# The cumulated decay of the SSD chunks: stored once per sequence and read back by broadcast, in place of matmuls

## The chip, the core and the metric

One NeuronCore of a Trainium2 chip runs the kernel. It has a matrix engine (TensorE, PE in the profile), a vector engine (VectorE, DVE), a scalar engine (ScalarE, ACT), GpSimd (POOL) and SyncE (SP), which here only issues transfers. Each engine runs its own list of instructions in order and waits on semaphores. SBUF is the on-chip memory of 128 partitions, PSUM holds 8 banks for the results of matmuls, and DRAM tensors lie outside. The metric is the time of one execution in microseconds of device time, less is better.

## The reference, cut to what matters

The model is one layer of an encoder on two sequences of 512 tokens: a mixing part (SSD heads, neighbourhood attention, pooling), cross attention and a mixture of experts. The change touches the SSD only, a scan over 4 chunks of 128 tokens per sequence, in both directions. For one direction:

```python
la = (dt * a).reshape(b, nc, L, G, R)
cs = jnp.cumsum(la, axis=2)
seg = cs[:, :, :, None] - cs[:, :, None, :]
decay = jnp.exp(jnp.where(tri[None, None, :, :, None, None], seg, -jnp.inf))
cb = jnp.einsum('bclgn,bcsgn->bclsg', cc, bc)
y_diag = jnp.einsum('bclsg,bclsgr,bcsgrp->bclgrp', cb, decay, xdt)
```

For every chunk, direction (2) and head (8), `decay` is a 128 by 128 matrix: the exponential of the cumulated sum at token l minus that at token s. The partitions of a tile hold s. So every partition needs the whole row of `cs` over l, for each head.

## The kernel before, in words

The program is one list of steps, `TL`, built by `timeline()`. Each engine walks the same list in the same order and issues its own part of each step, so an engine's order of work is fixed by the list. A step is a tuple: its kind, the sequence `s` and the chunk or tile.

The steps around the change:
- `dtv`, `dt`: from the projected time steps come `dts` and `la`, then by matmuls the cumulated sums `cs` (tokens on partitions) and totals `tot`. `la` is kept as two parts, `laH` and `laL`, whose sum it is.
- `sback`: the backward states, one step per chunk from the last one down.
- `sdec`: the decay matrices of one chunk. PE first makes the product of `bT` and `cT` (L1039). Then come 32 matmuls (L1047): with `laH` or `laL` of one head, repeated over 128 columns, as the stationary operand and a triangle of ones as the moving one, they leave the cumulated row of this head in every partition of a bank. 8 heads, 2 directions, 2 parts. DVE takes the smaller of that and its own partition's `cs` (L1899), writes `dec`, ACT applies `Exp` (L1530), DVE multiplies by the product `cbm` (L1907).
- `sy`: the output of the chunk. PE multiplies `dec` with `xdt` (L1077) into a bank; DVE adds the parts into `y1` (L1839 to L1875); ACT squares, POOL makes the reciprocal root (`yms`, `yrs`), DVE scales (L1879).
- `sout`: PE transposes, DVE scales into `y1` (L1914), POOL stores it to `mix_scratch`. The next chunk's L1839 waits for that store to land.

The chunks of the first sequence are interleaved with the projections `qk` of the second one, those of the second with the memory projections `mk`, `mv` and the output projection. Such a projection (GEMM in this text) is 24 matmuls of 512 columns on PE (L909 to L911); its `hn1` step is followed by a square on ACT, a sum on DVE (`hss`, L1730), a root on POOL (`hrs`) and a scaling on DVE (L1740). Weights come through `raw`: ACT rounds them into `Wh`, DVE makes the rest `Wl` (L1705).

Banks are given out in turn: each use takes the next of the 8, and PE waits until the use 8 before it is released. A `sdec` step has 6 uses, 4 of them for L1047.

POOL issues its DMAs on its own queue in the order of its steps: in `sdec` it multiplies `xs` with `dts` (`xdt`, L2343), loads the gate `zg` and makes `xw` (L740). The gate was stored in the `z` steps.

Of the kernel before, what the change touches and what calls it, by code (L numbers as in the profile page):

```python
# [23 lines left out]
P = 128  # L24
# [154 lines left out]
def bank_uses(step):  # L179
# [14 lines left out]
    if kind == "sdec":  # L194
        return 6
# [96 lines left out]
def encoder_layer(nc, dram, out):  # L292
# [3 lines left out]
    with ctx:  # L296
# [13 lines left out]
        mix_dram = nc.dram_tensor("mix_scratch", (NT, P, KT, P), F32).ap()  # L310
        z_dram = nc.dram_tensor("gate_scratch", (NT, P, D_INNER), F32).ap()
# [154 lines left out]
        stk.close()  # L466
        oneh_p = nc.alloc_sbuf_tensor_at("oneh_p", [P, 2 * NT, P], BF16, offset=at["raw0"])
# [77 lines left out]
        x_st = [sem(f"x_st{i}") for i in range(NT)]  # L545
# [76 lines left out]
        z_st = [sem(f"z_st{i}") for i in range(NT)]  # L622
# [14 lines left out]
        t_done = sem("t_done")  # L637
        y_done = sem("y_done")
# [267 lines left out]
        def _(pe):  # L906
# [39 lines left out]
            for step in TL:  # L946
# [67 lines left out]
                elif kind == "dt":  # L1014
# [17 lines left out]
                elif kind == "sdec":  # L1032
# [8 lines left out]
                    for dr in range(2):  # L1041
                        for hh in range(2):
                            b = take(pe, step, 2 + 2 * dr + hh)
                            for h in range(4):
                                e = dr * 8 + hh * 4 + h
                                for j, a in enumerate((laH, laL)):
                                    last = pe.matmul(b[:, h * P:(h + 1) * P], a[:, c, e:e + 1].to_broadcast([P, P]),  # L1047
                                                     tri_r[:, dr, :], start=j == 0, stop=j == 1)
                            last.then_inc(is_full(step, 2 + 2 * dr + hh), 1)
                elif kind == "sy":  # L1050
# [23 lines left out]
                    for h in range(SSD_H):  # L1074
                        hc = slice(h * SSD_P, (h + 1) * SSD_P)
                        for dr in range(2):
                            last = pe.matmul(b[:, hc], dec[:, dr, h, :], xdt[:, dr, hc], start=dr == 0, stop=dr == 1)  # L1077
# [251 lines left out]
        def _(act):  # L1329
# [34 lines left out]
            def stored(i):  # L1364

                for j in range(i, i + 4):
                    act.wait_ge(x_st[j], 16)
# [10 lines left out]
            for step in TL:  # L1378
# [19 lines left out]
                elif kind == "norm":  # L1398
# [18 lines left out]
                    if st == "ffn":  # L1417
                        act.dma_start(px_dram[i * P:(i + 1) * P, :], x_sb[:, i, :]).then_inc(x_st[i], 16)
# [105 lines left out]
                elif kind == "sdec":  # L1524
                    s, c = step[1], step[2]
                    for dr in range(2):
                        for hh in range(2):
                            wait_released(act, step, 2 + 2 * dr + hh)
                            for h in range(4 * hh, 4 * hh + 4):
                                last = act.activation(dec[:, dr, h, :], dec[:, dr, h, :], ACT.Exp,  # L1530
                                                      bias=ncs[:, dr, c, h:h + 1])
# [108 lines left out]
        def _(dve):  # L1640
# [49 lines left out]
            for step in TL:  # L1690
# [96 lines left out]
                elif kind == "z":  # L1787
                    k = nth(*step)
                    dve.wait_ge(zt_done, k + 1)
                    if k:  # L1790
                        dve.wait_ge(z_st[k - 1], 16)
# [21 lines left out]
                elif kind == "dt":  # L1813
                    k = nth(*step)
# [66 lines left out]
                elif kind == "sdec":  # L1881
# [10 lines left out]
                    if k:  # L1892
                        wait_full(dve, ("sy",) + chunks[k - 1], 0)
                    for dr in range(2):
                        for g in range(SSD_G):

                            j = 2 + 2 * dr + g
                            wait_full(dve, step, j)
                            tt(dec[:, dr, 4 * g:4 * g + 4, :], pb(step, j)[:, :].rearrange("p (h l) -> p h l", h=4),  # L1899
                               per_head(cs[:, dr, c, 4 * g:4 * g + 4], P), ALU.min).then_inc(is_free(step, j), 1)  # L1900
                    for g in range(SSD_G):
                        wait_released(dve, step, g)
                    for dr in range(2):
                        for g in range(SSD_G):
                            dve.wait_ge(e_done, 4 * k + 2 * dr + g + 1)
                            d = dec[:, dr, 4 * g:4 * g + 4, :]
# [315 lines left out]
        def _(pool):  # L2222
# [18 lines left out]

            pool.memset(neghalf[:, :], -0.5)
# [266 lines left out]
```

## Time and profile before

| what | us |
|---|---|
| median of 3 runs | 1236.51 (1230.76 to 1240.05) |
| the profiled execution, its own time | 1230.7 |
| its span | 1228.7 |
| PE busy | 1038.7 (85% of the span), 5029 instructions recorded |
| PE, loading of weights | 819.1 (67%) |
| DVE busy | 782.6 (64%) |
| ACT busy | 468.8 (38%) |
| POOL busy | 298.6 (24%) |

A busy share says how long an engine had something in work, not whether anybody waited for it. The profile also gives PE's granted clock (1.00 is 2.4 GHz, 0.50 is 1.2 GHz; mean 0.926 here), the share of the DMA engines, and for each instruction the idle time before it with what ended that time. "<-issue" means that nothing in the profile was waited for.

### The profile page before, as it was taken

The page shows a single profiled execution, that of the slowest core. Times are in us where ns is not written, and L with a number is a line of the kernel's source. Part 1 is how long each engine was busy: PE and PEld are TensorE (multiplying, and loading weights), DVE is VectorE, ACT ScalarE, POOL GpSimd, SP SyncE. Part 2 cuts the span into 40 slices and gives each one's busy share as a digit, 9 for nine tenths or more (in the row PEclk, how much of TensorE's full clock was granted, in tenths as well). Part 3 has the DMA queues.
Part 4 walks back from the last instruction along what each step waited for, and adds up shares of the span by engine and source line. Part 5 has one row for each costly group of instructions (what it writes and reads, how often), then busy time and mean ns, then how long its engine had stood idle before and what let it go on. Part 6 is the DMA issues. An engine that isn't in the chain of part 4 may idle for free.

```text
span 1228.7 us, 13980 instructions
## 1 busy us (share of the span) xinstructions
PE 1038.7 (85%) x5029; PEld 819.1 (67%) x5029; DVE 782.6 (64%) x1251; ACT 468.8 (38%) x849; POOL 298.6 (24%) x346
## 2 busy tenths in 40 slices
PE   1878978989797898999996999974999988898884
PEld 1746766867576677788875777764777666676662
DVE  4435766787566666774245466655898777877781
ACT  4222335233223523331113333323565655565560
POOL 1203402331340232110011111112244333232322
PEclk9988988879898896988988999976999999999998
DMA  5122223022122322433131001463699999899973
GB/s 190 37 70 84 77 96 122 18 70 78 60 78 86 117 73 86 146 103 129 60 91 35 35 35 52 163 282 125 224 367 367 362 354 355 348 360 361 347 281 102
DMA packets 65124, 197.40 MB, mean 161 GB/s; under 512 B 16608, under 2 KB 23168, under 8 KB 52640
## 3 DMA queue, kind: packets, MB, share of 16 engines
q1 hardware_dynamic: 43520, 151.14, 34.0%
q0 software_dynamic: 18688, 39.52, 9.0%
q10 hardware_dynamic: 2848, 5.84, 1.3%
q8 instruction: 41, 0.67, 0.2%
q14 instruction: 27, 0.22, 0.1%
HBM read 190.16 MB, written 37.75 MB: 185 GB/s over the span
## 4 chain that ended last, share of the span: by engine, by line
PE 44%; DVE 18%; issue 13%; DMA 11%; ACT 8%; POOL 6%; ACTq 1%; SPq 0%; DVEq 0%; POOLq 0%
DMA edr<-w_e_down 9%; PE bank L909 8%; PE bank L910 8%; PE bank L911 8%; DVE egl L1687 3%; PE gu_ps L909 2%; PE gu_ps L911 2%; PE gu_ps L910 2%; PE bank L959 2%; PE y_ps L1272 2%; DVE x_sb L1780 1%; DVE xn L1714 1%; DVE Wl L1705 1%; PE bank L1163 1%; ACT ghi L1362 1%
## 5 line engine op out<-in xcount | busy, mean ns | idle before, releaser
L909 PE MATMUL bank<-Wh,hTh 128*128 128x512 f32 x384 | 162.8, 424 | 4.6 <-issue 4.6
L910 PE MATMUL bank<-Wl,hTh 128*128 128x512 f32 x384 | 157.4, 410 | 0.0
L911 PE MATMUL bank<-Wh,hTl 128*128 128x512 f32 x384 | 156.7, 408 | 0.0
L1687 DVE TENSOR_TENSOR egl<-egr,ghi 128x2048 fp32r<-128x2048 f32 x64 | 144.1, 2291 | 14.9 <-ACT ghi L1362 14.9
L1362 ACT ACTIVATE ghi<-egr 128x2048 fp32r<-128x2048 f32 x64 | 119.6, 1931 | 0.0
L909 PE MATMUL gu_ps<-ghi,xgH 128*128 128x512 f32 x256 | 103.5, 404 | 1.4 <-DVE xgL L2054 1.4
L1705 DVE TENSOR_TENSOR Wl<-raw,Wh 128x1024 fp32r<-128x1024 f32 (+1 forms) x64 | 77.4, 1217 | 38.6 <-ACT Wh L1362 38.4
L911 PE MATMUL gu_ps<-ghi,xgL 128*128 128x512 f32 x256 | 100.7, 394 | 0.0
L910 PE MATMUL gu_ps<-egl,xgH 128*128 128x512 f32 x256 | 100.2, 392 | 0.0
L909 PEld LDWEIGHTS bank<-Wh,hTh 128*128 128x128 f32 x384 | 78.1, 203 | 22.6 <-issue 6.6
L911 PEld LDWEIGHTS bank<-Wh,hTl 128*128 128x128 f32 x384 | 76.9, 200 | 17.5
L910 PEld LDWEIGHTS bank<-Wl,hTh 128*128 128x128 f32 x384 | 77.4, 202 | 15.9
L1362 ACT ACTIVATE dhi<-edr 128x1024 fp32r<-128x1024 f32 x32 | 33.9, 1060 | 134.2 <-DMA edr<-w_e_down 118.0
L909 PE MATMUL bank<-hTh,Wh 128*128 128x512 f32 (+1 forms) x176 | 74.9, 425 | 9.2 <-issue 8.3
L1362 ACT ACTIVATE Wh<-raw 128x1024 fp32r<-128x1024 f32 (+1 forms) x64 | 63.1, 999 | 30.5 <-PE bank L911 19.6
L959 PE MATMUL bank<-ident,xn 128*128 128x128 f32 x160 | 29.5, 345 | 53.2 <-DVE xn L1714 53.2
L911 PE MATMUL bank<-hTh,Wl 128*128 128x512 f32 (+1 forms) x176 | 72.7, 413 | 0.0
L910 PE MATMUL bank<-hTl,Wh 128*128 128x512 f32 (+1 forms) x176 | 72.6, 413 | 0.0
L2059 DVE TENSOR_TENSOR edl<-edr,dhi 128x1024 fp32r<-128x1024 f32 x32 | 39.1, 1223 | 48.4 <-ACT dhi L1362 48.3
L2371 POOL DMA_INDIRECT pg<-partial_rows,idh x32 | 51.7, 1616 | 64.6 <-DMA partial_rows<-pg,idh 61.9
L2376 POOL DMA_INDIRECT partial_rows<-pg,idh x28 | 33.1, 1182 | 141.3 <-DVE pg L2079 141.3
L1272 PE MATMUL y_ps<-edr,hbF 128*128 128x512 f32 x128 | 65.3, 591 | 0.0
(309 smaller groups left out, 2190.6 us busy)
## 6 DMA issues: line engine op xcount, KB each, us to landing
egr<-w_e_gate SPq DMA_DIRECT2D x32, 1024.0 KB, 17.7
egr<-w_e_up SPq DMA_DIRECT2D x32, 1024.0 KB, 21.0
edr<-w_e_down SPq DMA_DIRECT2D x32, 1024.0 KB, 14.3
raw<-w_in SPq DMA_DIRECT2D x72, 256.0 KB, 3.0
raw<-w_xkv SPq DMA_DIRECT2D x16, 256.0 KB, 3.1
raw<-w_out SPq DMA_DIRECT2D x16, 256.0 KB, 3.2
raw<-mix_scratch SPq DMA_DIRECT2D x16, 256.0 KB, 3.4
partial_rows<-x_sb ACTq DMA_DIRECT2D x8, 512.0 KB, 2.7
```

The costliest lines, as they stand in the source:

```text
L909: pe.matmul(dst, ah, bh, start=first, stop=False)
L910: pe.matmul(dst, ah, bl, start=False, stop=False)
L911: return pe.matmul(dst, al, bh, start=False, stop=last)
L959: last = pe.transpose(b[:, j * P:(j + 1) * P], NORMED[st][0][:, f * P:(f + 1) * P], ident[:, :])
L1163: last = pe.matmul(b[:, j * 256:(j + 1) * 256], xqT[:, h, :], xkT[:, h, s * N_MEM:(s + 1) * N_MEM], start=True, stop=True)
L1272: last = pe.matmul(y_ps[:, c], hbF[:, :], edr[n % 3][:, 1, c], start=False, stop=True)
L1362: return act.activation(dst, src, ACT.Copy, **kw)
L1687: tt(egl[n % 4][:, a, :, :], egr[n % 4][:, a, :, :], ghi[n % 2][:, a, :, :].bitcast(F32), ALU.subtract)\
L1705: tt(lo, src, h, ALU.subtract).then_inc(w_low, 1)
L2059: tt(edl[n % 3][:, 0, :], edr[n % 3][:, 0, :], dhi[n % 2][:, 0, :].bitcast(F32), ALU.subtract)\
L2371: return pool.indirect_dma_start(out=to, out_offset=None, in_=table, in_offset=bass.IndirectOffsetOnAxis(ap=idx, axis=0), bounds_check=bou ...
L2376: return pool.indirect_dma_start(out=table, out_offset=bass.IndirectOffsetOnAxis(ap=idx, axis=0), in_=frm, in_offset=None, bounds_check=bo ...
```

## The change

The cumulated sums are produced a second time, now with heads on partitions, and travel through DRAM.
- `dt`: four more matmuls (128 columns each) leave the cumulated rows of all 4 chunks, 8 heads and one direction in 64 partitions. DVE copies them to `y1`, POOL stores them to `decay_scratch` (64 KB).
- `sdec`: the 32 matmuls and their 4 banks are gone. One DMA from POOL per chunk (`load_decay`) reads the chunk's 16 rows of 128 numbers and writes them to all 128 partitions of a tile, 8 KB a partition, 1 MB in all. Two tiles `decays` alternate; the second lies over `prob`, which the neighbourhood attention uses at other times. DVE's `min` now works in place on that tile.
- POOL issues the loads of chunks 0 and 1 in the step `sback` of chunk 1, the loads of chunks 2 and 3 in `sdec` of chunks 1 and 2, ahead of `xdt`.
- Semaphores of the stores of `z` and of the rows for the experts are shared by two tiles each, so that there are enough of them.

```diff
@@ bank_uses
     if kind == "sdec":
-        return 6
+        return 2
@@ encoder_layer
+        cs_dram = nc.dram_tensor("decay_scratch", (SEQS, 2, TPS * 2 * SSD_H, P), F32).ap()
+        decays = [dec, nc.alloc_sbuf_tensor_at("dec1", [P, 2, SSD_H, P], F32, offset=at["prob"])]
@@ PE, dt
+                    for dr in range(2):
+                        for j, a in enumerate((laH, laL)):
+                            last = pe.matmul(b[0:64, 128 + dr * P:256 + dr * P], a[:, :, :].rearrange("p c h -> p (c h)"),
+                                             tri_r[:, dr, :], start=j == 0, stop=j == 1)
                     last.then_inc(is_full(step), 1)
@@ PE, sdec
-                    for dr in range(2):
-                        for hh in range(2):
-                            b = take(pe, step, 2 + 2 * dr + hh)
-                            for h in range(4):
-                                e = dr * 8 + hh * 4 + h
-                                for j, a in enumerate((laH, laL)):
-                                    last = pe.matmul(b[:, h * P:(h + 1) * P], a[:, c, e:e + 1].to_broadcast([P, P]),
-                                                     tri_r[:, dr, :], start=j == 0, stop=j == 1)
-                            last.then_inc(is_full(step, 2 + 2 * dr + hh), 1)
@@ DVE, dt
+                    if s:
+                        dve.wait_ge(ssd_st[s - 1], 16 * TPS)
+                    dve.tensor_copy(y1[0:64, 0:2 * P], b[0:64, P:3 * P]).then_inc(cst_done, 1)
@@ DVE, sdec
-                    if k:
-                        wait_full(dve, ("sy",) + chunks[k - 1], 0)
+                    dve.wait_ge(dec_ld[c % 2], 16 * (k // 2 + 1))
                     for dr in range(2):
                         for g in range(SSD_G):
-
-                            j = 2 + 2 * dr + g
-                            wait_full(dve, step, j)
-                            tt(dec[:, dr, 4 * g:4 * g + 4, :], pb(step, j)[:, :].rearrange("p (h l) -> p h l", h=4),
-                               per_head(cs[:, dr, c, 4 * g:4 * g + 4], P), ALU.min).then_inc(is_free(step, j), 1)
+                            d = decays[c % 2][:, dr, 4 * g:4 * g + 4, :]
+                            tt(d, d, per_head(cs[:, dr, c, 4 * g:4 * g + 4], P), ALU.min).then_inc(min_done, 1)
@@ POOL
+            def load_decay(s, c):
+
+                rows_of = bass.AP(cs_dram.tensor, (P * s + 2 * SSD_H * c) * P, [[0, P], [(64 + SSD_H) * P, 2], [1, SSD_H * P]])
+                pool.dma_start(decays[c % 2][:, :, :, :].rearrange("p d h l -> p d (h l)"), rows_of)\
+                    .then_inc(dec_ld[c % 2], 16)
@@ POOL, steps
+                elif kind == "dt":
+                    pool.wait_ge(cst_done, step[1] + 1)
+                    pool.dma_start(cs_dram[step[1]].rearrange("d r l -> r d l"),
+                                   y1[0:64, 0:2 * P].rearrange("p (d l) -> p d l", d=2)).then_inc(cs_st, 16)
...
-                elif kind == "sback" and step[2] > 1:
-                    decayed(pool, step[1], 1, step[2] - 1, per_head, heads)
+                elif kind == "sback":
+                    s, c = step[1], step[2]
+                    if c > 1:
+                        decayed(pool, s, 1, c - 1, per_head, heads)
+                    else:
+                        if s:
+                            wait_full(pool, ("sy", s - 1, TPS - 1), 0)
+                        pool.wait_ge(cs_st, 16 * (s + 1))
+                        load_decay(s, 0)
+                        wait_full(pool, ("nav", s, 3))
+                        load_decay(s, 1)
...
+                    if 0 < c < TPS - 1:
+                        load_decay(s, c + 1)
```

What stands on POOL before chunk 0 of the first sequence: the load of `gain`, the root `hrs` of the projection norm, then the step's own work. Before:

```order
L2261 DMA gain<-norm_mem 128x1024
L2233 TENSOR_SCALAR hms<-hss 128x8
L2234 TENSOR_TENSOR hrs<-hms,neghalf 128x8
L2343 TENSOR_TENSOR xdt<-x_sb,dts 128x512 x2
L2346 DMA x_sb<-gate_scratch 128x512
L740 TENSOR_TENSOR xw<-x_sb,wst 128x512
```

And now, in the numbering of the changed kernel (`dec_49` is the second tile):

```order
L2269 DMA gain<-norm_mem 128x1024
L2235 TENSOR_SCALAR hms<-hss 128x8
L2236 TENSOR_TENSOR hrs<-hms,neghalf 128x8
L2247 DMA dec<-decay_scratch 128x2x1024
L2247 DMA dec_49<-decay_scratch 128x2x1024
L2366 TENSOR_TENSOR xdt<-x_sb,dts 128x512 x2
L2369 DMA x_sb<-gate_scratch 128x512
L746 TENSOR_TENSOR xw<-x_sb,wst 128x512
```

The two loads stand behind `hrs` and ahead of `xdt`. The second place on POOL is chunk 2 of the first sequence, behind the root `yrs` of chunk 1. Before:

```order
L2233 TENSOR_SCALAR yms<-yss 128x2
L2234 TENSOR_TENSOR yrs<-yms,neghalf 128x2
L2343 TENSOR_TENSOR xdt<-x_sb,dts 128x512 x2
L2346 DMA x_sb<-gate_scratch 128x512
L740 TENSOR_TENSOR xw<-x_sb,wst 128x512
```

Now:

```order
L2235 TENSOR_SCALAR yms<-yss 128x2
L2236 TENSOR_TENSOR yrs<-yms,neghalf 128x2
L2247 DMA dec_49<-decay_scratch 128x2x1024
L2366 TENSOR_TENSOR xdt<-x_sb,dts 128x512 x2
L2369 DMA x_sb<-gate_scratch 128x512
L746 TENSOR_TENSOR xw<-x_sb,wst 128x512
```

The load of chunk 3 came in between `yrs` and `xdt`. The third place is PE at chunk 1 of the second sequence. Now the product of `bT` and `cT`, the transposes of chunk 0's output and the next GEMM follow each other:

```order
L977 MATMUL bank<-ident,qn 128x128 x8
L1049 MATMUL bank<-x_sb 128x128 x2
L1084 MATMUL bank<-ident,y 128x128 x4
L915 MATMUL bank<-Wh,hTh 128x512
L916 MATMUL bank<-Wl,hTh 128x512
```

Before, the 32 matmuls of L1047 stood between the second and the third of these rows, ending so:

```order
L1047 MATMUL bank<-tri_r,laH 128x128
L1047 MATMUL bank<-tri_r,laL 128x128
L1083 MATMUL bank<-ident,y 128x128 x4
L909 MATMUL bank<-Wh,hTh 128x512
L910 MATMUL bank<-Wl,hTh 128x512
```

The GEMM moved up by these 32 instructions.

## Rows read from the trace of the kernel before

**Rows 1.** Two stretches: us, busy us (instructions) of PE, PEld, DVE, ACT, POOL; clock; DMA
```profile
205.00:320.00 115.00, 101.33 (x556) 80.47 (x557) 83.46 (x177) 34.63 (x100) 32.23 (x41) 0.88 0.22 65
420.00:560.00 140.00, 129.05 (x653) 106.55 (x652) 97.82 (x166) 46.00 (x111) 30.71 (x40) 0.88 0.31 102
```

**Rows 2.** What is recorded on line 1047, and who waited for it (us, times)
```profile
L1047 PE MATMUL bank<-tri_r,laH x128: 272/274/476, 214.7 to 544.3; 128*128 128x128 f32 x128
...
  DVE dec L1899: 2.8, 3
```

**Rows 3.** PE in order of time, first chunk: start, us, instruction, idle before
```profile
214.69 0.33 PE L1047 MATMUL bank<-tri_r,laH 128*128 128x128 f32 x1
...
218.21 0.27 PE L1047 MATMUL bank<-tri_r,laL 128*128 128x128 f32 x1
...
227.81 4.91 PE L1077 MATMUL bank<-xdt,dec 128*128 128x64 f32 x32 [1.24 <-DVE dec L1907]
```

**Rows 4.** DVE in order of time, first sequence
```profile
221.52 2.48 DVE L1899 TENSOR_TENSOR dec<-bank,cs 128x512 f32<-128x512 f32 x4
...
227.06 0.69 DVE L1907 TENSOR_TENSOR dec<-dec,cbm 128x512 f32<-128x512 f32 x1 [0.47 <-ACT dec L1530]
...
240.61 0.61 DVE L1879 TENSOR_SCALAR y<-y,yrs 128x256 f32<-128x256 f32 x2 [2.04 <-POOL yrs L2234]
241.14 0.68 DVE L1730 TENSOR_REDUCE hss<-sqb 128x8 f32<-128x512 f32 x1
...
246.13 2.47 DVE L1899 TENSOR_TENSOR dec<-bank,cs 128x512 f32<-128x512 f32 x4
...
266.50 2.17 DVE L1879 TENSOR_SCALAR y<-y,yrs 128x256 f32<-128x256 f32 x2 [2.04 <-POOL yrs L2234]
```

**Rows 5.** POOL in order of time, first sequence
```profile
215.26 1.67 POOL L2234 TENSOR_TENSOR hrs<-hms,neghalf 128x8 f32<-128x8 f32 x1
...
246.91 1.06 POOL L740 TENSOR_TENSOR xw<-x_sb,wst 128x512 f32<-128x512 f32 x1
...
266.44 2.08 POOL L2343 TENSOR_TENSOR xdt<-x_sb,dts 128x512 f32<-128x512 f32 x2
```

**Rows 6.** DMA issues from 205 to 222 us: count, KB each, median us to landing
```profile
gain<-norm_mem POOLq DMA_DIRECT2D x1, 512.0 KB, 5.2
...
x_sb<-gate_scratch POOLq DMA_DIRECT2D x1, 256.0 KB, 3.1
```

**Rows 7.** Tile egr: all 64 loads of 1 MB, issue to landing
```profile
DMA to landing us min/median/max: 4.8/18.2/24.3
```

**Rows 8.** PE in order of time, second sequence
```profile
482.21 0.78 PE L909 MATMUL bank<-Wh,hTh 128*128 128x512 f32 x1
...
522.57 6.01 PE L1077 MATMUL bank<-xdt,dec 128*128 128x64 f32 x32 [3.36 <-DVE dec L1907]
...
552.52 5.32 PE L1077 MATMUL bank<-xdt,dec 128*128 128x64 f32 x32 [1.26 <-DVE dec L1907]
```

**Rows 9.** DVE in order of time, second sequence
```profile
450.49 2.48 DVE L1899 TENSOR_TENSOR dec<-bank,cs 128x512 f32<-128x512 f32 x4
...
481.72 0.69 DVE L1899 TENSOR_TENSOR dec<-bank,cs 128x512 f32<-128x512 f32 x1 [1.02 <-PE bank L1047]
...
491.41 1.23 DVE L1705 TENSOR_TENSOR Wl<-raw,Wh 128x1024 fp32r<-128x1024 f32 x1 [5.55 <-ACT Wh L1362]
492.55 0.42 DVE L1839 TENSOR_TENSOR y<-bank,ecs 128x256 f32<-128x256 f32 x1
...
565.10 0.69 DVE L1977 TENSOR_TENSOR x_sb<-x_sb,bank 128x512 f32<-128x512 f32 x1 [2.01 <-PE bank L911]
```

**Rows 10.** POOL in order of time, second sequence
```profile
442.40 1.01 POOL L2234 TENSOR_TENSOR hrs<-hms,neghalf 128x4 f32<-128x4 f32 x1
...
486.15 0.59 POOL L2359 DMA_DIRECT2D mix_scratch<-y  x1 [9.14 <-DVE y L1914]
```

**Rows 11.** PE in order of time, after the `dt` step
```profile
194.11 1.97 PE L959 MATMUL bank<-ident,xn 128*128 128x128 f32 x8 [2.42 <-DVE xn L1714]
```

More of the change, by code:

```diff
@@ L544, in encoder_layer @@
         count_done = sem("count_done")
-        x_st = [sem(f"x_st{i}") for i in range(NT)]
+        x_st = [sem(f"x_st{i}") for i in range(TPS)]
         eg_ld = [[sem(f"eg_ld{i}{a}") for a in range(2)] for i in range(4)]
@@ L621, in encoder_layer @@
         zg_done = sem("zg_done")
-        z_st = [sem(f"z_st{i}") for i in range(NT)]
+        z_st = [sem(f"z_st{i}") for i in range(TPS)]
         z_ld = sem("z_ld")
@@ L637, in encoder_layer @@
         t_done = sem("t_done")
+        cst_done = sem("cst_done")
+        cs_st = sem("cs_st")
+        dec_ld = [sem(f"dec_ld{i}") for i in range(2)]
+        min_done = sem("min_done")
         y_done = sem("y_done")
@@ L1076, in _ @@
                         for dr in range(2):
-                            last = pe.matmul(b[:, hc], dec[:, dr, h, :], xdt[:, dr, hc], start=dr == 0, stop=dr == 1)
+                            last = pe.matmul(b[:, hc], decays[c % 2][:, dr, h, :], xdt[:, dr, hc], start=dr == 0, stop=dr == 1)
                     last.then_inc(is_full(step, 0), 1)
@@ L1417, in _ @@
                     if st == "ffn":
-                        act.dma_start(px_dram[i * P:(i + 1) * P, :], x_sb[:, i, :]).then_inc(x_st[i], 16)
+                        if i >= TPS:
+                            act.wait_ge(x_st[i - TPS], 16)
+                        act.dma_start(px_dram[i * P:(i + 1) * P, :], x_sb[:, i, :]).then_inc(x_st[i % TPS], 16)
                 elif kind == "hT" and step[1] == "ffn":
@@ L1527, in _ @@
                         for hh in range(2):
-                            wait_released(act, step, 2 + 2 * dr + hh)
+                            act.wait_ge(min_done, 4 * nth(*step) + 2 * dr + hh + 1)
                             for h in range(4 * hh, 4 * hh + 4):
-                                last = act.activation(dec[:, dr, h, :], dec[:, dr, h, :], ACT.Exp,
-                                                      bias=ncs[:, dr, c, h:h + 1])
+                                d = decays[c % 2][:, dr, h, :]
+                                last = act.activation(d, d, ACT.Exp, bias=ncs[:, dr, c, h:h + 1])
                             last.then_inc(e_done, 1)
@@ L1813, in _ @@
                 elif kind == "dt":
-                    k = nth(*step)
+                    k, s = nth(*step), step[1]
                     wait_full(dve, step)
@@ L2336, in _ @@
                     k = nth(*step)
-                    pool.wait_ge(z_st[k], 16)
-                    pool.wait_ge(z_st[s * TPS + TPS - 1], 16)
+                    pool.wait_ge(z_st[c], 16 * (s + 1))
+                    pool.wait_ge(z_st[TPS - 1], 16 * (s + 1))
                     if k:
@@ L2407, in _ @@
             for i in range(NT):
[L2408 removed]
+                pool.wait_ge(x_st[i % TPS], 16 * (i // TPS + 1))
             gather_rows(2)
```

9 lines of the change are left out of this document (4 added, 5 removed).

## The prediction, made before the changed kernel ran

> **What bounds the kernel now.** I read the busy table of two stretches first: 205 to 320 us, where the first sequence's SSD chunks run, and 420 to 560 us, where the second's do [rows 1]. PE is busy 101.3 of 115.0 and 129.1 of 140.0 us there, DVE 83.5 and 97.8. That looks like PE as the bound, and the change takes PE work away. So the next view asks who waits for that work. Line 1047 holds 256 matmuls (two groups of 128), and in the whole execution DVE waits for them 2.8 us, in three pieces [rows 2]. Then I follow one chunk in order of time. The 32 matmuls of chunk 0 start between 214.69 and 218.21, 0.11 us apart. PE later reaches L1077, sits idle 1.24 us for DVE's L1907, and starts at 227.81, right when DVE's last L1907 ends (227.06 + 0.69) [rows 3, 4]. From 221.52 to 241.14 no idle time of DVE is put down to PE: its gaps are 0.47 us for ACT's exponentials and 2.04 us for ACT's squares and POOL's square root [rows 4]. So in the first sequence each chunk is one long chain DVE, ACT, POOL, DVE, in DVE's fixed order, and PE fills the time beside it. Taking work from PE there buys idle PE.
>
> **What is removed.** At that spacing, 3.52 us for 31 steps, the 256 matmuls take at least 29 us of PE. On the path are only the places where DVE waits. All are in chunk 1 of the second sequence. L1899 waits for line 1047 three times, 2.8 us in all, the last time 1.02 [rows 2, 9]. With these waits gone, L1907 will wait for ACT twice as in chunk 0, 0.47 us each [rows 4], which it doesn't there now: 1.8 us are left. Behind the same matmuls stands the GEMM that starts at 482.21 [rows 8]. It starts about 6 us earlier without them (they run at the low clock there, and DVE's `Wl` becomes its wait), so ACT's `Wh` comes earlier and DVE's wait of 5.55 us before 491.41 closes [rows 9]. What is late next is the store of `y1`: issued at 486.15 [rows 10], now 1.8 earlier, at 484.3; with 3.1 us to landing, as another 256 KB on this queue [rows 6], it lets L1839 start at 487.4, where it starts at 492.55 now [rows 9]. Gain: **5.2 us**.
>
> **What is added, and where it is hidden.** The four extra matmuls and DVE's copy of the cumulated decay in the `dt` step cost nothing. The transpose behind them has 2.42 us idle before it, waiting for `xn` [rows 11], and four matmuls of 128 columns at 0.11 to 0.21 us are under 0.9. If the cover were gone, each of the two steps would cost that. The store of `decay_scratch` has over 10 us until its first reader. `min` reads SBUF in place of PSUM with the same 512 elements a partition: nothing by itself.
>
> **The first load of each sequence.** It stands on POOL behind the square root `hrs` of the projection norm. In the first sequence that ends at 215.26 + 1.67 = 216.93 [rows 5], and DVE wants the tile at 221.52 [rows 4]: 4.6 us. In the second it ends at 443.41 [rows 10] and DVE wants it at 450.49 [rows 9]: 7.1 us. No row shows a broadcast of 1 MB on POOL's queue. The nearest is `gain`, the same 4 KB row to 128 partitions, 512 KB, 5.2 us to landing; a 256 KB load takes 3.1 [rows 6]. Going on at that slope gives 9.4. From below, the fastest 1 MB load, plain and on SP's queue, took 4.8 [rows 7]. I take 7.0, nearer to the broadcast row plus 512 KB at its pace. Then DVE waits **2.4 us** in the first sequence (0.2 to 4.8) and **0** in the second (0 to 2.3). The loads of chunks 1 to 3 are issued some 20 us before use. As a page has it (the Trainium skill, "DMA: Bandwidth & Descriptors", section "Anatomy of one DMA — SWDGE (gpsimd) path"), a transfer costs about 2.0 us plus its bytes at 436 GB/s, 4.4 us for 1 MB as an estimate. By that the first wait would be nil and the sum 2.4 us lower.
>
> **PE's clock.** With more idle time before L1077, PE will run it low. L1077 took 4.91 us after 1.24 us of idling [rows 3], 5.32 after 1.26, but 6.01 after 3.36 [rows 8]. After the change PE idles there for 1.24 us, the 3.5 of the matmuls and the wait for the load, 5 to 7 us. This costs where the path goes on through PE: in chunk 0 the GEMM behind L1077 feeds ACT and then L1730 at 241.14, which follows L1879 (240.61 + 0.61) without a gap [rows 4]; ACT's square before it waited for that GEMM, so I count no slack. I take 6.0: **1.1 us** in the first sequence, 0.9 in the second's chunk 0, and 0.7 in its chunk 3, where L1977 at 565.10 waits for PE [rows 9]. From below 0; from above, 32 steps at half the pace of 0.11 us (7.0) give 2.1, 1.9 and 1.7.
>
> **POOL and DVE beside each other.** A DVE instruction can be held up by POOL: two L1879 take 0.61 us at 240.61, but 2.17 at 266.50, where POOL's `xdt` starts at 266.44 [rows 4, 5]. In chunk 2 the new load's issue (about 0.6 us, as 486.15 shows [rows 10]) stands between `yrs` and `xdt`, so L1879 runs free: 1.6 us back in each sequence. But DVE meets `xdt` and `xw` one instruction later. I take half, **0.8 us gained** each (0 to 1.6). In chunk 1 `xdt` and `xw` move 0.6 us later, onto L1899. Today L1899 takes 2.47 us at 246.13 with `xw` beside it [rows 4, 5], as much as the 2.48 without it at 221.52: by this row the price is nil. But its source was a bank, and L1879's, in SBUF, was held up 1.6. So 0 to 2 us; I take **1.0** in each sequence. The Trainium skill ("SBUF — State Buffer", section "Who interferes with whom") says that a DVE instruction with two SBUF inputs contends with a GpSimd instruction that reads SBUF, and one with at most one does not (outside certain modes). It speaks against this change, since L1899 gets a second SBUF input. By the rule the 1.0 stays, by the row of L1899 alone the sum would be 2.0 lower.
>
> **The sum.** First sequence: 2.4 + 1.1 + 1.0 - 0.8 = +3.7. Second: 0.9 + 1.0 - 5.2 - 0.8 + 0.7 = -3.4. Together +0.3 us: 29 us of PE time or more leave and the span stays. What follows hangs on the chain and moves along. Against the profiled run's own time, 1230.7 us (span 1228.7), this is 1231.0. The median of the runs shown, 1236.5, is 5.8 above that run, so I say 1236.8, about **1237**. All lower ends: first -1.4, second -5.2 - 1.6 = -6.8, so 1228.3. All upper ends: first 4.8 + 2.1 + 2.0 = 8.9; second 2.3 + 1.9 + 2.0 - 5.2 + 1.7 = 2.7, so 1248.1.
>
> **The rivals.**
> - Load in time: the load lands within 4.8 us and the clock costs nothing. For it: SP's fastest 1 MB. Against: the broadcast row with half the bytes took longer. Sum about -8: 1228.
> - PE's time is on the path after all: 29 us come off, 1208. For it: PE is busy for 88 and 92% of the stretches. Against: 2.8 us of waiting in all.
> - Slower, by one mechanism: the broadcast read. All 128 partitions fetch the same 8 KB, and if these reads queue up, the load lands late at both first chunks. Each us beyond 7 costs one in each sequence, so the kernel is 1% slower from 13 us to landing: 1249. For it: no row of this size. Against: `gain`'s 5.2 us.
>
> **How the numbers follow.** The forecast has 0.58, load in time 0.18, PE on the path 0.08, a queueing broadcast 0.16. About 1%, 12.4 us, is what a measurement of this kernel can tell from no change. PE on the path gives faster, with a share of the load in time: 0.11. The slow load passes 1% for most of its chance: 0.14. The rest, 0.75, is within 1%. The runs shown lie between 1230.8 and 1240.1, so a median moves by a few us as well: 1227 to 1249 takes in both sums of ends and leaves out what is beyond 1% on either side.
>
> **What would show it.** In the new profile: L1899 of chunk 0 waits for a DMA, 2 to 3 us in the first sequence and near none in the second; L1077 takes 6 us or more in most chunks; the share of PE falls by over 2 points with the span as it was; the L1879 behind the load of chunk 3 takes 0.6 us; the 5.55 us before L1705 is gone. The prediction is wrong if the stretch from 205 to 320 us gets shorter, if DVE waits for later loads too, or if DVE's time for L1899 grows by more than 1 us a chunk.

## The result and the profile after

The changed kernel takes 1239.8 us (median of 20 runs, 1236.0 to 1246.1), the kernel before, measured beside it, 1233.4 us (20 runs, 1225.6 to 1241.8). The ratio is 1.0054, 95% interval 1.0031 to 1.0076. A second measurement of 12 runs gave 1.0052 (1.0029 to 1.0074). So the change costs about 6 us: half a per cent, less than the 1% below which I counted it as no change, and yet real.

| | before | after |
|---|---|---|
| span of the profiled execution, us | 1228.7 | 1239.3 |
| PE busy, us | 1038.7 | 1018.4 |
| DVE busy, us | 782.6 | 792.5 |
| POOL busy, us | 298.6 | 319.7 |
| mean granted clock | 0.926 | 0.909 |

PE lost 20 us of busy time and the span got longer. The same stretches as in [rows 1], in the kernel after (us, busy us of PE, PEld, DVE, ACT, POOL, clock, DMA share, GB/s):

```profile
205.00:320.00 115.00, 85.11 (x399) 65.02 (x399) 87.49 (x173) 33.64 (x98) 32.82 (x43) 0.79 0.29 95
420.00:560.00 140.00, 114.23 (x526) 91.91 (x527) 101.87 (x173) 48.79 (x118) 35.46 (x47) 0.85 0.40 139
```

PE has 16.2 us less in the first stretch, at a clock of 0.79 in place of 0.88. DVE has 4.0 us more. It has the same arithmetic, but for one small copy per sequence that lies ahead of this stretch, so something holds its instructions up. To find where, I put the two traces side by side by DVE's order and took, for each of its instructions, start after minus start before. That difference is -1.86 us at 204 us (mostly chance: a second trace of the same kernel before stands at -1.99 there), +5.2 at 320, +4.9 at 430 and +4.3 at 600. So 7.1 us are lost in the first sequence's chunks, and 0.7 won in the second's. The steps of the difference stand at few instructions. DVE after, first sequence (start, us, instruction; lines are 2 to 6 higher than before):

```profile
215.73 3.20 DVE L1867 TENSOR_TENSOR S_b<-S_b,edec 64x256 f32<-64x256 f32 x2
...
221.04 2.48 DVE L1902 TENSOR_TENSOR dec<-dec,cs 128x512 f32<-128x512 f32 x4
...
242.58 0.69 DVE L1733 TENSOR_REDUCE hss<-sqb 128x8 f32<-128x512 f32 x1 [1.86 <-ACT sqb L1452]
...
245.91 3.13 DVE L1708 TENSOR_TENSOR Wl<-raw,Wh 128x544 fp32r<-128x544 f32 x1
...
270.16 4.55 DVE L1885 TENSOR_SCALAR y<-y,yrs 128x256 f32<-128x256 f32 x2 [2.04 <-POOL yrs L2236]
```

The same `S_b` and `Wl` in the kernel before:

```profile
217.57 1.84 DVE L1861 TENSOR_TENSOR S_b<-S_b,edec 64x256 f32<-64x256 f32 x2
...
244.47 0.95 DVE L1705 TENSOR_TENSOR Wl<-raw,Wh 128x544 fp32r<-128x544 f32 x1
```

(`S_b` is the backward state, L1885 the scaling by `yrs`.) `S_b` takes 1.36 us more, `hss` waits 1.86 for ACT where it waited for nothing [rows 4], `Wl` takes 2.18 more, and the scaling ahead of chunk 2 4.55 in place of 2.17 [rows 4]. These four make 7.8 us. L1902, the `min`, waits for no load and takes its 2.48 us. (The first load landed at 220.03, 4.98 us after its issue. Without the longer `S_b` DVE would have been at L1902 at about 219.7, so some 0.3 us of waiting is hidden behind it.) POOL after, at the same places:

```profile
215.05 1.51 POOL L2247 DMA_DIRECT2D dec<-decay_scratch  x2
216.59 2.05 POOL L2366 TENSOR_TENSOR xdt<-x_sb,dts 128x512 f32<-128x512 f32 x2
...
245.22 0.79 POOL L2247 DMA_DIRECT2D dec<-decay_scratch  x1
246.03 2.05 POOL L2366 TENSOR_TENSOR xdt<-x_sb,dts 128x512 f32<-128x512 f32 x2
...
270.09 0.78 POOL L2247 DMA_DIRECT2D dec<-decay_scratch  x1
270.90 2.05 POOL L2366 TENSOR_TENSOR xdt<-x_sb,dts 128x512 f32<-128x512 f32 x2
...
273.50 1.05 POOL L746 TENSOR_TENSOR xw<-x_sb,wst 128x512 f32<-128x512 f32 x1
```

Each DVE instruction that got longer began while POOL was issuing a load: 215.73, 245.91 and 270.16 lie inside 215.05 to 216.56, 245.22 to 246.01 and 270.09 to 270.87. The last one ends when `xw` does (274.71 and 274.55). Before, `xdt` came straight behind the root and began ahead of these instructions (243.79, with `Wl` at 244.47); there POOL took the delay, 2.53 us for `xdt`, and `Wl` took 0.95:

```profile
243.79 2.53 POOL L2343 TENSOR_TENSOR xdt<-x_sb,dts 128x512 f32<-128x512 f32 x2
```

PE after, ahead of the first sequence's wait, and at the end of the second (start, us, instruction, idle before):

```profile
227.32 7.09 PE L1078 MATMUL bank<-xdt,dec 128*128 128x64 f32 x32 [4.86 <-DVE dec L1909]
...
555.16 6.37 PE L1078 MATMUL bank<-xdt,dec 128*128 128x64 f32 x32 [3.19 <-DVE dec L1909]
```

It took 4.91 after 1.24 us of idling, and 5.32 after 1.26 [rows 3, 8]. DVE after, second sequence:

```profile
475.86 0.69 DVE L1733 TENSOR_REDUCE hss<-sqb 128x4 f32<-128x512 f32 x1 [1.04 <-ACT sqb L1452]
...
478.56 3.63 DVE L1708 TENSOR_TENSOR Wl<-raw,Wh 128x1024 fp32r<-128x1024 f32 x1
...
493.23 1.23 DVE L1708 TENSOR_TENSOR Wl<-raw,Wh 128x1024 fp32r<-128x1024 f32 x1 [1.08 <-ACT Wh L1363]
494.87 0.42 DVE L1845 TENSOR_TENSOR y<-bank,ecs 128x256 f32<-128x256 f32 x1 [0.41 <-DMA mix_scratch<-y]
...
503.83 3.55 DVE L1885 TENSOR_SCALAR y<-y,yrs 128x256 f32<-128x256 f32 x2 [2.06 <-POOL yrs L2236]
...
569.35 0.69 DVE L1979 TENSOR_TENSOR x_sb<-x_sb,bank 128x512 f32<-128x512 f32 x1 [3.64 <-PE bank L917]
```

The wait of 5.55 us [rows 9] is 1.08. The difference falls from +8.05 behind the long `Wl` to +2.32 at L1845: 5.7 us won, the only gain above 2 us. The losses beside it: 1.0 (`hss`), 2.2 (`Wl`), 1.4 (L1885), 1.6 (L1979, 3.64 against 2.01).

### The profile page after: what moved, and what is told of

It is laid out like the page before. It is cut to its first block, busy times and chain, and to the rows that moved or that the text cites. A ratio compares the mean times of both kernels' runs of the same rounds, so it can differ in the third digit from the quotient of the medians.

```text
span 1239.3 us, 13491 instructions
## 1 busy us (share of the span) xinstructions
PE 1018.4 (82%) x4781; PEld 798.6 (64%) x4781; DVE 792.5 (64%) x1253; ACT 468.6 (38%) x849; POOL 319.7 (26%) x356
## 4 chain that ended last, share of the span: by engine, by line
PE 46%; DVE 16%; issue 12%; DMA 11%; ACT 7%; POOL 6%; ACTq 0%; SPq 0%; DVEq 0%; POOLq 0%
DMA edr<-w_e_down 9%; PE bank L915 9%; PE bank L916 8%; PE bank L917 8%; DVE egl L1690 3%; PE gu_ps L915 2%; PE gu_ps L917 2%; PE gu_ps L916 2%; PE bank L965 2%; PE y_ps L1273 2%; PE bank L1078 2%; DVE x_sb L1783 1%; DVE xn L1717 1%; DVE Wl L1708 1%; PE bank L1164 1%
## 5 line engine op out<-in xcount | busy, mean ns | idle before, releaser
L1708 DVE TENSOR_TENSOR Wl<-raw,Wh 128x1024 fp32r<-128x1024 f32 (+1 forms) x64 | 82.1, 1291 | 32.5 <-ACT Wh L1363 32.3
L2394 POOL DMA_INDIRECT pg<-partial_rows,idh x32 | 66.5, 2079 | 73.3 <-DMA partial_rows<-pg,idh 70.6
L1078 PE MATMUL bank<-xdt,dec 128*128 128x64 f32 x256 | 45.9, 363 | 26.0 <-DVE dec L1909 26.0
```

Source lines behind the costliest of these rows:

```text
L1078: last = pe.matmul(b[:, hc], decays[c % 2][:, dr, h, :], xdt[:, dr, hc], start=dr == 0, stop=dr == 1)
L1708: tt(lo, src, h, ALU.subtract).then_inc(w_low, 1)
L2394: return pool.indirect_dma_start(out=to, out_offset=None, in_=table, in_offset=bass.IndirectOffsetOnAxis(ap=idx, axis=0), bounds_check=bou ...
```

## The theories and the experiments

Theory A: POOL's loads and the `xdt` and `xw` that they push back hold up DVE, some 9 us over both sequences (1.4, 2.2 and 2.4 in the first, 2.2 and 1.4 less 0.6 given back in the second; the text on record has the same five terms and says 8). Theory B: the lost matmuls let PE's clock fall, and this costs the 6 us. Theory C: the loads land late or crowd other transfers. A variant's time is its ratio to the kernel before on the same chip. Its place in the trace is the same difference of DVE's starts against the first trace of before, from 204 to 600 us, so that what happens ahead of and behind the changed part is left out. That is not little: behind 600 us the second trace of the kernel before loses 3.9 us against the first, and the variants' traces lose 1.3 to 11.9, two traces of the same kernel up to 5 us apart. So the ratio, from 11 to 20 runs, decides on the time, and the trace only on where something happens.

| kernel | ratio (95%) | 204 to 600 us, in the trace |
|---|---|---|
| changed | 1.0054 (1.0031 to 1.0076) | +6.1 |
| changed, again | 1.0052 (1.0029 to 1.0074) | +6.1 |
| loads behind `xw` | 1.0010 (0.9987 to 1.0032) | -3.4 |
| the same, again | 0.9985 (0.9959 to 1.0011) | -0.7 |
| loads from ACT | 0.9980 (0.9957 to 1.0004) | -3.2 |
| the same, again | 0.9993 (0.9965 to 1.0021) | 0.0 |
| matmuls kept, loads added | 1.0047 (1.0024 to 1.0071) | +4.7 |
| loads behind `xw`, fill | 0.9993 (0.9965 to 1.0021) | -1.1 |
| hybrid, one load | 0.9939 (0.9918 to 0.9961) | -8.9 |
| hybrid, again | 0.9926 (0.9904 to 0.9947) | -8.4 |
| hybrid, two loads | 0.9955 (0.9927 to 0.9983) | -3.4 |
| hybrid, load ahead | 0.9956 (0.9932 to 0.9980) | -7.9 |

### The changed kernel again

> The changed kernel once more, as the measure for the three that run beside it: about 1.005 of the kernel before. In its trace both theories expect again what the first one showed in the first sequence: the state add L1867 of chunk 0 at about 3.2 us (1.84 before), Wl L1708 of chunk 1 at about 3.1 us (0.95 before), the addition L1885 ahead of chunk 2 at about 4.5 us (2.2 before).

1.0052, and the same picture in the trace: `S_b` 3.20 us at 216.25, and +6.1 us between 204 and 600.

### The loads moved behind `xdt` and `xw` on POOL

```diff
@@ POOL, sback
                     if c > 1:
                         decayed(pool, s, 1, c - 1, per_head, heads)
-                    else:
+                    if c == 2:
...
                         load_decay(s, 0)
-                        wait_full(pool, ("nav", s, 3))
-                        load_decay(s, 1)
@@ POOL, sdec
-                    if 0 < c < TPS - 1:
-                        load_decay(s, c + 1)
...
                     if c < TPS - 1:
                         decayed(pool, s, 0, c, per_head, heads)
+                        if c == 0:
+                            wait_full(pool, ("nav", s, 3))
+                        load_decay(s, c + 1)
```

> The loads of the decays stay on GpSimd, but are issued elsewhere: the first of a sequence in the step of state chunk 2, the others behind xdt and xw of the chunk before, so that no load stands ahead of an xdt. Theory A (GpSimd's displaced xdt and xw hold up VectorE): the terms +1.4 (S_b of chunk 0), +2.2 (Wl of chunk 1) and +2.4 (L1885 ahead of chunk 2) of the first sequence go, and +2.2 and +1.4 of the second, in all some 8 us: 0.993 to 0.994 of the changed kernel, which is 0.998 to 1.000 of the kernel before; in its trace S_b takes 1.8, Wl about 1.0 and L1885 about 2.2 us. Theory B (the lower clock of TensorE, with less work for it, costs the 6 us): nothing changes, 1.004 to 1.006 of the kernel before, and the waits of hss for ScalarE in chunk 0 stay at 1.9 and 1.0 us. Theory C (the loads land late or take bandwidth from others): a load issued later lands later, and the time rises.

1.0010, and 0.9985 in a second measurement. DVE in this kernel, first sequence:

```profile
238.79 0.69 DVE L1733 TENSOR_REDUCE hss<-sqb 128x8 f32<-128x512 f32 x1 [0.89 <-ACT sqb L1452]
...
242.12 0.95 DVE L1708 TENSOR_TENSOR Wl<-raw,Wh 128x544 fp32r<-128x544 f32 x1
...
243.79 3.62 DVE L1902 TENSOR_TENSOR dec<-dec,cs 128x512 f32<-128x512 f32 x4
...
264.70 2.17 DVE L1885 TENSOR_SCALAR y<-y,yrs 128x256 f32<-128x256 f32 x2 [2.03 <-POOL yrs L2236]
```

`S_b` (1.84), `Wl` and L1885 have their durations of before, in the second sequence too. All 256 matmuls are still gone and all eight loads still run, so neither can be what costs the 6 us by itself; moving the eight issues is worth 0.4 to 0.7%, where A expected 0.6 to 0.7. What stays is that the change does not gain: `hss` still waits, 0.89 here and 2.47 us at 469.29. And a new row shows up: L1902 takes 3.62 us with `xw` (244.59) beginning in the middle of it. In the kernel before `xw` falls on this instruction too, which then takes 2.47 [rows 4, 5]; there one of its two inputs is a bank, here both lie in SBUF.

### The loads issued from ACT's queue

```diff
-                pool.dma_start(decays[c % 2][:, :, :, :].rearrange("p d h l -> p d (h l)"), rows_of)\
+                act.dma_start(decays[c % 2][:, :, :, :].rearrange("p d h l -> p d (h l)"), rows_of)\
                     .then_inc(dec_ld[c % 2], 16)
```

> The loads are issued from ScalarE's queue, in the same steps as in the changed kernel, and GpSimd has its order of before, but for the one store of the cumulated sums per sequence. Theory A (GpSimd's displaced operations): as with the loads put behind xdt, 0.998 to 1.000 of the kernel before, less what the issues cost ScalarE, where they stand in its own path (unknown, up to 0.8 us each if as long as on GpSimd, of which two per sequence stand behind exponentials). Theory B (clock): 1.004 to 1.006. Theory C (transfers): as the changed kernel, 1.005.

0.9980, later 0.9993: the other way to leave POOL's order alone gives the same. (The first pair was 0.003 apart, 1.0010 and 0.9980; measured again side by side it was 0.0008, 0.9985 and 0.9993, so the queue makes no difference that shows.) The loads land after 4.4 to 7.7 us here (median 5.8; 5.0 to 7.7, median 5.3, in the changed kernel).

### Matmuls kept, loads added

```diff
 def bank_uses(step):
     if kind == "sdec":
-        return 2
+        return 6
@@ DVE, sdec
-                            tt(d, d, per_head(cs[:, dr, c, 4 * g:4 * g + 4], P), ALU.min).then_inc(min_done, 1)
+                            j = 2 + 2 * dr + g
+                            wait_full(dve, step, j)
+                            tt(d, pb(step, j)[:, :].rearrange("p (h l) -> p h l", h=4),
+                               per_head(cs[:, dr, c, 4 * g:4 * g + 4], P), ALU.min).then_inc(is_free(step, j), 1)
```

> The matmuls L1047 of before are kept and the minimum reads their bank as before; the loads are issued on GpSimd where the changed kernel has them, into tiles that the minimum then overwrites. So this is the cost of the loads and of the second cumulated sum without the gain and without the lower clock. Theory A: +6 us in the first sequence (S_b +1.4, Wl +2.2, L1885 +2.4) and +3.6 in the second (Wl +2.2, L1885 +1.4), with nothing gained at chunk 1: 1.006 to 1.009 of the kernel before. Theory B: the clock is that of before and the loads cost nothing: 1.000 to 1.001.

1.0047, under the 1.006 to 1.009 of A and far from the 1.000 of B; the loads, with the copy and the store that feed them, cost as much as the whole change, with all matmuls in place. `Wl` takes 3.13 and 3.63 us, L1885 4.56 and 3.55, as in the changed kernel. The `hss` wait that I had put down to the missing matmuls is there too in the first sequence:

```profile
228.87 6.18 PE L1087 MATMUL bank<-xdt,dec 128*128 128x64 f32 x32 [2.60 <-DVE dec L1921]
```

```profile
243.66 0.69 DVE L1742 TENSOR_REDUCE hss<-sqb 128x8 f32<-128x512 f32 x1 [1.38 <-ACT sqb L1461]
```

POOL's displacement works through PE as well: the 1.36 us that `S_b` loses are 1.36 us more of idling for PE (2.60, before 1.24), the matmuls run longer (6.18, before 4.91), and ACT and `hss` wait. In the second sequence, where `S_b` loses nothing, `hss` waits for nothing here.

### The loads moved, and matmuls put back

```diff
+                        for h in range(16):
+                            pe.matmul(b[:, P:2 * P], laH[:, c, h:h + 1].to_broadcast([P, P]), tri_r[:, g, :], start=True, stop=True)
                         pe.matmul(b[:, 0:P], bT[r, tok], cT[r, tok], start=True, stop=True)\
```

(The text on record has two numbers wrong. The moving operand has 128 columns, not 64x128. And 32 matmuls were removed per chunk, not 64: 256 in eight chunks [rows 2]. The fill has 2 times 16 of the same shape, 256 in its trace as well, so TensorE does all of the removed work again, not half. They stand ahead of the product of `bT` and `cT`; the removed ones stood behind it.)

> The kernel with the loads behind xdt and xw, and 32 matmuls of 64x128 columns per chunk put back on TensorE at the place of the removed 64, with their result unused, so that TensorE does half of the removed work again. If the waits of hss for ScalarE that were left in it (0.97 and 0.57 us in the first sequence, 2.5 us at chunk 0 of the second, by the starts on VectorE against the kernel before) come from the lower clock after the idle time, they shrink to under 0.5 us each, and the wait ahead of Wl in chunk 1 of the second sequence comes back in part, +2.6 us of the 5.7 gained; the sum is then the same as without the fill, within 1 us. If they come from somewhere else (the loads, ScalarE's order), the hss waits stay at 2.5 us and the time goes up by the 2.6 us.

0.9993. PE in this kernel, and the sum behind it on DVE:

```profile
225.71 3.79 PE L1080 MATMUL bank<-xdt,dec 128*128 128x64 f32 x32 [0.74 <-DVE dec L1911]
...
454.49 5.16 PE L1080 MATMUL bank<-xdt,dec 128*128 128x64 f32 x32 [2.08 <-DVE dec L1911]
```

```profile
467.68 0.69 DVE L1735 TENSOR_REDUCE hss<-sqb 128x4 f32<-128x512 f32 x1
```

The same places without the fill:

```profile
453.56 7.09 PE L1078 MATMUL bank<-xdt,dec 128*128 128x64 f32 x32 [4.86 <-DVE dec L1909]
```

```profile
469.29 0.69 DVE L1733 TENSOR_REDUCE hss<-sqb 128x4 f32<-128x512 f32 x1 [2.47 <-ACT sqb L1452]
```

Useless matmuls remove a wait of 2.47 us. So B is true as a mechanism: PE's idling before L1078 costs DVE time two steps later. In exchange the gain at chunk 1 goes, all of it, not the 2.6 us I had expected for half of the work: from 469 us to L1845 of chunk 1 this kernel loses 0.4 us, while the unfilled one wins 3.2 (5.7 less the 2.5 of `hss`). DVE now waits there for the product that the fill stands in front of:

```profile
475.69 0.49 DVE L1898 TENSOR_TENSOR cbm<-bank,tri_r 128x128 f32<-128x128 f32 x2 [1.89 <-PE bank L1051]
480.02 0.49 DVE L1898 TENSOR_TENSOR cbm<-bank,tri_r 128x128 f32<-128x128 f32 x2 [3.84 <-PE bank L1051]
```

The ratios are level, 0.9993 against 1.0010 and 0.9985.

### The hybrid: one chunk loaded, seven by matmul

From where DVE waited for L1047 before, only chunk 1 of the second sequence can gain, so only it reads its decay by a load, issued behind `xw` of chunk 0.

```diff
+LOADED = [(1, 1)]
 def bank_uses(step):
     if kind == "sdec":
-        return 2
+        return 2 if step[1:] in LOADED else 6
@@ POOL, sdec, behind xw
-                        load_decay(s, c + 1)
+                        if (s, c + 1) in LOADED:
...
+                            load_decay(s, c + 1)
```

> The matmuls stay in seven of the eight chunks, and only chunk 1 of the second sequence reads its decay by a load (issued behind xw of chunk 0; one load and one store in the whole kernel). Theory A: it keeps the gain of -5.7 us at chunk 1 of the second sequence and none of the costs, so VectorE is 5 to 6 us ahead of the kernel before at 600 us, with hss of chunk 0 waiting no longer than before, and the time is 0.995 to 0.997 of the kernel before. Theory B (the gain at chunk 1 is given back by a clock that falls there): hss or the additions L1979 behind it wait 2 us or more, and the time is 0.998 to 1.000.

0.9939, and 0.9926 in a second measurement, against 0.995 to 0.997 expected: 7 to 10 us faster than the kernel before, some 14 to 16 faster than the changed one. DVE is 8.9 us ahead at 600 us, not 5 to 6. Chunk 1 gives 5.7 again. Of the other 3.2 the largest piece, 1.9 (2.1 in the second hybrid trace), came at one place, 565 us. The stretch in the kernel before, and in the second hybrid run:

```profile
550.00:575.00 25.00, 22.21 (x102) 18.39 (x101) 11.96 (x24) 4.54 (x12) 2.07 (x4) 0.86 0.19 67
```

```profile
550.00:575.00 25.00, 23.25 (x105) 18.87 (x105) 10.69 (x20) 4.17 (x9) 1.52 (x3) 1.00 0.41 148
```

The wait of 2.01 us before L1977 [rows 9] is gone at the full clock. To see whether that is chance I took a second trace of the kernel before.

> The kernel before once more, for a second trace. The hybrid is 2.4 us further ahead behind 560 us, where the first trace of the kernel before has a wait of 2.01 us ahead of L1977 at a clock of 0.86 and the hybrid none at 1.00. If this is the hybrid's doing, the second trace shows the wait again; if it is chance (the same kernel differed by 2.6 and 3.2 us in this stretch in two of the variants), it shows another value. The waits ahead of chunk 1 of the second sequence (5.55 us for Wh) and the durations of S_b, Wl and L1879 should be those of the first trace within 0.3 us.

It shows 2.01 us again, at 0.86, and 5.63 us for `Wh`, and from 204 to 600 us it is within 1 us of the first. So the hybrid has the full clock there in both of its traces and the kernel before in none. All 14 traces fall into two groups at this place. Where PE idled 0.04 us at most before the 32 matmuls of chunk 3 (both hybrid traces, the matmuls kept, the fill, the load ahead), they took 3.8 us, the clock from 550 to 575 us is 1.00 and L1977 waits 0.13 us at most. In the other nine PE idled 1.07 to 3.94 us, they took 4.93 to 7.01, the clock is 0.80 to 0.91 and L1977 waits 2.01 to 3.69. The hybrid:

```profile
545.30 3.79 PE L1091 MATMUL bank<-xdt,dec 128*128 128x64 f32 x32
```

Why PE does not idle there, 60 us behind the only chunk that differs, isn't settled: kernels that are quite unlike are in the first group, and no run here moves that alone.

> The hybrid once more, as the measure for the two beside it, and to see whether its 0.994 holds: between 0.992 and 0.996.

### The hybrid with chunk 0 of the second sequence loaded too

```diff
-LOADED = [(1, 1)]
+LOADED = [(1, 0), (1, 1)]
```

> The hybrid with chunk 0 of the second sequence loaded too (in the step of state chunk 2), so its 64 matmuls go as well; no load stands ahead of an xdt. If the matmuls of chunk 0 hold TensorE's clock up for the matmuls behind them, the wait of hss for ScalarE ahead of chunk 1, 0 in the hybrid and 2.47 us where all chunks are loaded, comes back at about 2.5 us and the time is 0.002 above the hybrid's 0.994: 0.996. If the hss wait has another cause (the sum over all chunks, an order), it stays at 0 and the time is that of the hybrid.

0.9955. The wait comes back, but at 0.99 us and not 2.5, though PE idles and slows exactly as where all chunks are loaded:

```profile
456.20 7.09 PE L1091 MATMUL bank<-xdt,dec 128*128 128x64 f32 x32 [4.86 <-DVE dec L1932]
```

```profile
470.46 0.69 DVE L1749 TENSOR_REDUCE hss<-sqb 128x4 f32<-128x512 f32 x1 [0.99 <-ACT sqb L1465]
```

So the idling is the cause, and the price behind it depends on when the clock comes back: with all chunks loaded behind `xw` it is 0.50 from 452.0 to 465.7 us and `hss` waits 2.47, here it is 0.50 from 455.0 to 465.2 and `hss` waits 0.99, behind the same 7.09. Of the 5 us by which this kernel falls behind the hybrid up to 600 us, 1.0 is at this wait, and 3.9 come between 540 and 565 us, at the additions (L1977 in the kernel before): from 550 to 575 us the clock is 0.86 here, 1.00 in the hybrid. So the 0.996 expected came out, but only 1.0 us of it by the wait it was expected from. (This one trace is of the slowest execution of this kernel, 1237.1 us against a median of 1229.8.)

### The hybrid with its load where the change has it

```diff
@@ POOL, sback
                     if c > 1:
                         decayed(pool, s, 1, c - 1, per_head, heads)
+                    elif s:
...
+                        load_decay(s, 1)
```

> The hybrid with its only load issued where the changed kernel has it, in the step of state chunk 1, ahead of chunk 0's xdt on GpSimd, instead of behind xw. Theory A (a load issued ahead of an xdt costs VectorE time through the displaced xdt and xw): Wl of chunk 1 takes longer than its 1.45 us, up to the 3.63 us of the changed kernel, where two loads stood ahead; +0.7 us if the delay counts once for each load, +2.2 us if the overlap decides: 0.9945 to 0.996 of the kernel before. If the place of the issue does not matter, Wl stays at 1.45 us and the time at 0.994.

0.9956, 4 us above the hybrid beside it. My theory had the right mechanism and the wrong instruction. `Wl` of chunk 1 stays at 1.45: what stands ahead of *its* `xdt` in the changed kernel is the load of chunk 2. Held up is the `Wl` ahead of chunk 0's `S_b`:

```profile
442.38 3.63 DVE L1724 TENSOR_TENSOR Wl<-raw,Wh 128x1024 fp32r<-128x1024 f32 x1
```

```profile
441.70 0.78 POOL L2270 DMA_DIRECT2D dec<-decay_scratch  x1
442.51 2.05 POOL L2384 TENSOR_TENSOR xdt<-x_sb,dts 128x512 f32<-128x512 f32 x2
```

With one load ahead, `Wl` takes 3.63 and `S_b` 1.71 (1.45 and 2.95 without it): 0.9 us in all. With two loads ahead, as in the changed kernel, `xdt` misses `Wl` and nothing is lost at this place. One load can cost more than two. The trace accounts for at most 1 us of the 4 (7.9 us ahead at 600, the hybrids 8.9 and 8.4). The two intervals, 0.9932 to 0.9980 and 0.9904 to 0.9947, overlap, so that the time came out as expected doesn't show the theory right; the 3.63 does.

## Why the prediction was right and where it was not

The time, 1237, was 3 us under the 1239.8 measured, and inside the range. Much of that is luck. The median of three runs from which I started, 1236.5, was 3 us above the 1233.4 of twenty, and the change itself, +0.3 in my sum, is +6; the one error covers half of the other. What the kernel does to DVE I had wrong in most terms.

- **PE is not on the path**: right. I took 29 us of matmuls or more away; PE's busy time fell by 20, since matmuls that stayed ran longer, as L1077 shows. Only the waits in chunk 1 of the second sequence gave more than 2 us. (DVE has a third gap between 221.52 and 241.14, 0.67 us for POOL's `hrs` at 230.43, which I passed over; it changes no term.)
- **Gain there, 5.2**: right, 5.7 at L1845, bounded by the store of `y1` as foreseen (0.41 us for `mix_scratch`).
- **Copy and extra matmuls, 0**: right. Between 320 and 430 us the difference moved by 0.3.
- **First load, 2.4**: wrong. The eight loads landed in 5.0 to 7.7 us (median 5.3), the first of each sequence in 4.98 and 5.29, and DVE waited for none, in the first sequence only because `S_b` held it up for longer than the 0.3 us that, by my estimate from the starts, were missing. Half of the bytes took 5.2 [rows 6]: a slope drawn from 256 and 512 KB didn't hold to 1 MB. The 4.4 us estimated from the Trainium skill ("DMA: Bandwidth & Descriptors", section "Anatomy of one DMA — SWDGE (gpsimd) path") came nearer to the median than my 7.0, though it is below the fastest of the eight. The wait that follows from it, nil, is what the trace shows.
- **PE's clock, 1.1 + 0.9 + 0.7**: right in place, too small. Measured 1.9, 1.0 and 1.6, together 4.5 for my 2.7. I took 6.0 us for L1077; it took 7.09, the upper bound, since PE idled 4.86 us. In the first sequence part of it is POOL's doing, as the run with the matmuls kept shows.
- **L1879 runs free beside the load's issue, -0.8 in each sequence**: this is the step that failed. It went to 4.55 and 3.55 us, +2.4 and +1.4. I took a DMA issue on POOL for an instruction that leaves DVE alone. L1885 needs 0.6 us and began 0.74 before `xdt` in both sequences (270.16 and 503.83); beside the issue it did not finish.
- **L1899 held up, +1.0 in each**: right instruction for the wrong kernel. In the changed kernel `xw` did not fall on it, 2.48 to 2.53 us. Where it does, with the loads moved, it takes 3.62, and with the source in a bank and `xw` as much beside it 2.47 (the hybrid): 1.15 us. That is what the Trainium skill says ("SBUF — State Buffer", section "Who interferes with whom"): two inputs in SBUF contend with GpSimd's reads, one doesn't, outside certain modes. By that rule I should have looked at every DVE instruction with two such inputs that a moved `xdt` can meet; I looked at one. `Wl` and `S_b` have two. L1885 has one tensor as input and is held up as well, 4.55 us here and 2.17 beside `xdt` before, so the count of inputs alone isn't enough.
- **What I left out**: `S_b` +1.4 and `Wl` +2.2 in the first sequence, `Wl` +2.2 in the second. I moved POOL's work by 0.6 us in my head; the loads' issues took 0.72 to 0.79, and two of them, 1.51 us, stand ahead of chunk 0's `xdt`. And I asked only where `xdt` would land, not what would have begun ahead of it.

POOL's terms were +0.4 in my sum. They are 5.9 in the first sequence (1.4 + 2.2 + 2.4) and 3.0 in the second (2.2 + 1.4, less 0.6 that the next `hTl` gives back): 8.5 more than I had. With 1.8 more for the clock, 2.4 less for the load and 0.5 more of gain that is +7.4, where the trace has 5.8 more than my sum; small gains on the way, 0.5 at `Wh` of chunk 2, 0.5 at `S_b` of the second sequence and 0.3 between the sequences among them, make most of the rest. Neither a queueing broadcast nor PE's time on the path came true. Of the rival "load in time" the first half did, and not the second: the clock cost 4.5 us. Its sum on record, -8, is wrong too: with the load at 0.2 and the clock at 0 my terms give -4.6; -8 is the sum of all lower ends. The rival that should have stood there was POOL holding up DVE.

Of the signs I named, three came: L1077 takes 6 us or more in five of the eight chunks, PE's share falls by 2.4 points (though the span grew), and the 5.55 us before L1705 shrank to 1.08. Two did not: L1902 waits for no DMA, and L1885 does not take 0.6 us.

## What to carry over

An instruction or a DMA issue put ahead of another engine's work is not priced by its own 0.8 us, but by what its neighbours then meet: list, for each place, which engine begins first, and every instruction within a few microseconds that has two inputs in SBUF or that a row already shows held up, as L1879 was. Take work from an engine only where somebody waits for it; of eight chunks one was worth changing, and changing that one alone gave 0.6 to 0.7% where changing all cost 0.5%. And an idle matrix engine isn't free: after 3 to 8 us of idling its next matmuls ran at the lower clock here, and whoever waited for them paid.

## What was not expected of the hardware

- Who begins first matters. `xdt` ahead of `Wl` by 0.7 us: `Wl` 0.95, `xdt` 2.53. `Wl` ahead of `xdt` by 0.12 us, with a load's issue before: `Wl` 3.13, `xdt` 2.05. For the wider `Wl` of the second sequence 1.45 and 3.02 against 3.63 and 2.05. For the two scalings of 128x256 that began 0.07 us behind a load's issue, 4.55 us against 0.61 alone. That the issue itself takes part is shown by these (they would have ended before `xdt` began), and by the first of the two `S_b` of the changed kernel. It ran beside nothing but the two issues, ended at 216.52 as the second did (216.57) and took 0.78 us; the same instruction with POOL at rest took 0.42 (in the kernel with the load ahead):

```profile
215.73 0.78 DVE L1867 TENSOR_TENSOR S_b<-S_b,edec 64x256 f32<-64x256 f32 x1
```

```profile
447.22 0.42 DVE L1883 TENSOR_TENSOR S_b<-S_b,edec 64x256 f32<-64x256 f32 x1
```

  For `Wl` the runs don't part the issue from the order.
- The same 32 matmuls of 64 columns took 3.79 us after 0.74 us of idling, 4.91 after 1.24, 6.18 after 2.60 and 7.09 after 4.86. The idling just before does not set it alone: they also took 5.15 after 2.56 (the kernel before, at 456.76 us) and 7.09 after 3.02 (loads behind `xw`, at 250.64). Around the 7.09 of the changed kernel's first chunk the granted clock is 0.50, the lower level, 1.2 GHz; the stretch in the changed kernel:

```profile
225.00:235.00 10.00, 7.68 (x34) 7.59 (x35) 8.25 (x20) 2.56 (x8) 1.86 (x2) 0.50 0.13 30
```

- A broadcast of 1 MB from 8 KB of DRAM to 128 partitions landed in a median of 5.3 us issued by POOL in the changed kernel, 6.3 with the issues moved, and 5.8 issued by ACT, where one issue took 0.37 us and not 0.78.
